# Moving operands of U, query and V at other addresses, and a shorter first ranking round

## The chip, the cores and the metric

The kernel runs on one core of a Trainium2 chip. The metric is device time in microseconds of one execution, the median of three runs. The result is one array of 256 tokens by 1024 features in float32.

## The reference, cut to what matters

Two transformer blocks run one after the other on 256 tokens of width 1024. Each ends in a PEER layer, and that is where the change lies:

```
qh = (t @ w_q).reshape(T, 8 heads, 2, 128)
s = einsum(qh, sub_keys)                       # 128 scores for each head and half
s_top, i_top = top_k(s, 16)
cand = s_top[..., 0, :, None] + s_top[..., 1, None, :]
best, pos = top_k(cand.reshape(..., 256), 16)
idx = i_top[0] * 128 + i_top[1]  at pos        # 16384 experts
g = softmax(best)
act = gelu(einsum(u_tab[idx], t))
y = einsum(g * act, v_tab[idx])
```

The second block does the same with its own tables and shared sub-keys. The rest (modulation, windowed attention, short convolution, latent attention, gated linear attention) is not touched.

## The kernel before, in words

The kernel doesn't gather experts. It multiplies all 16384 rows of U with all tokens, takes Gelu, multiplies by a dense matrix of gates that is zero for experts not chosen, and multiplies by all of V. A stage is made of units: 16 for the query (`wq`), 128 for U, 128 for V, each 512 KB of weights that SyncE streams into a ring of four slots. The two blocks are called b = 1 and b = 2.

Every float32 product is made from two float32r parts. The weights of a unit are split in halves of 512 columns: ScalarE casts the high part into `hl[:, slot, 0]` (L2321 in U, L2651 in V), VectorE subtracts to get the low part into `hl[:, slot, 1]` (L2324, L2661). `hl` has four such slots (HLRING), so two units. The tokens' parts are `hsplit` for U, `shifted_raw` (b = 1) or `raw_split` (b = 2) for the query, and `csplit` for V, whose slots (CRING = 4) hold the gated activations of one unit each. `hl` holds the stationary operand, the others the moving one.

`passes` (L937 to L939) multiplies high by high, low weights by high, and high weights by low, 256 columns each. A unit of U has eight feature blocks k, so 24 matmuls. `wide_passes` (L2245, L2246) does V: the high weights stream both parts of a `csplit` slot at once as 512 columns, then the low weights stream the high part, 256 columns. A unit of V has eight such pairs.

A partition's addresses are counted here in words of 4 bytes. `gbuf` begins at word 44064. `hl` begins there; `hsplit` and `csplit` share the space from word 48160 on. Remainders of the word address by 64:

```
                           high part   low part    stationary
hsplit (U)                    32          16           32   (hl)
raw_split (query, b = 2)      32          16           32   (hl)
csplit (V), slots 0 and 2     32          16           32   (hl)
csplit (V), slots 1 and 3      0          48           32   (hl)
h_parts (fill1, block 1)      32          32           32   (whi_front, ring_lo, s_lo)
mixed_hi, mixed_lo (w_out)    16          16           32   (whi_a, ring_lo)
```

Steps inside a tensor (256 words from one k to the next, 128 from one stationary block to the next) leave these remainders as they are. A slot of `csplit` is 608 words long: 256 high, 48 empty, 256 low, 48 empty.

The order of the work in U: VectorE does the low splits, and after each half unit n it calls `between(n)` (L2796), which does one step of the ranking. There are four rounds of 52 steps: 36 steps of top-k (`topk_part`) and 16 of lookup (`lookup_part`). ScalarE's Exp of a round's gates has a unit of its own in `exp_at` (L2744). The first two rounds end with `picks_ready`; for each, GpSimd then scatters 64 columns of gates to HBM, one indirect DMA at a time (L2478). TensorE turns the chosen experts at unit 105 (`TURN_UNIT`), and VectorE takes them at half unit `TAKE_SLOT` = 214. From unit 111 on, the gates of the other tokens are built with one-hot matmuls (L2554).

SyncE's queue (`peer_loads`) holds, in this order: the loads of U's units, each behind the split that frees its ring slot; the first four loads of V (L2864); a wait for the whole scatter; the first four loads of gates into `gring` (L2879); and then V's loads and gates in turn. In V, VectorE multiplies the activations by the gates (L2593), ScalarE casts the high part into `csplit` (L2649), VectorE subtracts the low part (L2655).

Of the kernel before, what the change touches and what calls it, by code (L numbers as in the profile page):

```python
# [24 lines left out]
F32R = mybir.dt.float32r  # L25
# [5 lines left out]
P = 128  # L31
D = 1024
KD = D // P
T = 256
# [16 lines left out]
HALF = UNIT // 2  # L51
HLRING = 4
CRING = 4
# [210 lines left out]
def build(nc, stream, xc, metaT, vectors, common, consts1, consts2, keys1, keys2, w_a2, out):  # L264
# [5 lines left out]
    def place(name, shape, dtype=F32, at=None):  # L270
        size = math.prod(shape[1:])
        where = top[0] if at is None else at
        t = nc.alloc_sbuf_tensor_at(name, shape, dtype, offset=4 * where)
        if at is None:
            top[0] += (size + 7) // 8 * 8
        return t, where

    ring, ring_at = place("ring", [P, RING, UNIT])
    ring_lo, _ = place("ring_lo", [P, RING, UNIT], F32R, at=ring_at)
    resid, _ = place("resid", [P, KD, T])  # L280
    s_area, s_at = place("s_area", [P, NT * HEADS * 2 * P])
    arena, arena_base = place("arena", [P, P * T])
    gbuf, gbuf_at = place("gbuf", [P, 10240])
    keybuf, keybuf_at = place("keybuf", [P, 2 * P])
    tmpbuf, _ = place("tmpbuf", [P, 2 * P])
    zeros, _ = place("zeros", [P, ZEROS])
    _, late_rest_at = place("late_rest", [P, 4 * P])

    hl, _ = place("hl", [P, HLRING, 2, HALF], F32R, at=gbuf_at)
    SHIFT = 48  # L290
    hpair, _ = place("hsplit", [P, 2, KD * T + SHIFT], F32R, at=gbuf_at + 2 * HLRING * HALF)
    hsplit = hpair[:, :, 0:KD * T].rearrange("p x (k t) -> p x k t", k=KD)
    cpair, _ = place("csplit", [P, CRING, 2, T + SHIFT], F32R, at=gbuf_at + 2 * HLRING * HALF)
    csplit = cpair[:, :, :, 0:T]
    vec_at, n_vec = offsets(VECS)
    con_at, n_con = offsets(CONSTS)
    vec, _ = place("vec", [P, n_vec])
    con, _ = place("con", [P, n_con])
    mod, _ = place("mod", [P, 48, 2])
    scale1, _ = place("scale1", [P, KD, 2])  # L300
    scale2, _ = place("scale2", [P, KD])
    small, _ = place("small", [P, 32])
    half_gate, _ = place("half_gate", [P, KD])
    twice_w, _ = place("twice_w", [P, 2, KD])
# [195 lines left out]
    acts = arena  # L500

    K = Space(gbuf, 10240)
    K.take(8192 + 2 * SHIFT)
    picks_best, gates = K.take(4, 64), K.take(4, 64)
    pos_f, rank1, rank2 = K.take(64), K.take(64), K.take(64)
    key_f, chosen = K.take(2, 64), K.take(2, 2 * 64)
# [307 lines left out]
    tiles[group_of["out1"][-KD]].each = ("mixed1_split",)  # L814

    h_full = gbuf[:, 8192:10240].rearrange("p (k t) -> p k t", k=KD)
    rpair, _ = place("raw_split", [P, 2, KD * T + SHIFT], F32R, at=s_at)
    raw_split = rpair[:, :, 0:KD * T].rearrange("p x (k t) -> p x k t", k=KD)
    ffn_root = n2[:, 0, 0:T]
    token_root = small[:, 26:28]  # L820

# [1428 lines left out]
    ITEMS = 4  # L2250
    ROUNDS = NT * HEADS // ITEMS
    ITEM_SLOTS, LOOK_SLOTS = 9, 16
    ROUND_SLOTS = ITEMS * ITEM_SLOTS + LOOK_SLOTS
    EXP_LAG = 2
    TURN_UNIT = ROUNDS * ROUND_SLOTS // 2 + 1
    TAKE_SLOT = 2 * TURN_UNIT + 4

# [194 lines left out]
    def take_turned(dve, b):  # L2452

        dve.wait_ge(S("experts_turned"), b)
        dve.tensor_copy(sel[:, 0:3, :], ps[:, 4, 0:3 * P].rearrange("p (c t) -> p c t", c=3))
        dve.tensor_scalar(sel[:, 3:5, :], ps[:, 4, P:3 * P].rearrange("p (c t) -> p c t", c=2), -1.0, None, ALU.mult)\
           .then_inc(S("sel_taken"), 1)
# [265 lines left out]
    def peer_act(act, b):  # L2723

        for s in range(UB):
            u_unit("act", act, b, 0, s, first=True, table="wq", ready=EARLY)
            if s == 2:
                entries[b].act_root(act)
        for s in range(UB):
            u_unit("act", act, b, 1, s, table="wq")  # L2730
            for k in (2 * s, 2 * s + 1):
                entries[b].act_high(act, k)
        u_loop("act", act, b, 2, NQ // UB, table="wq")
        early_hi(act, b, 0, "u")
        early_hi(act, b, 1, "u")
        if b == 2:
            take_unit(act, b, NQ // UB, -2, table="wq")
        early_hi(act, b, 2, "u")
        if b == 2:
            take_unit(act, b, NQ // UB, -1, table="wq")  # L2740
        early_hi(act, b, 3, "u")
        peer_act_scores(act, b)
        load_gelu(act, b)
        exp_at = {(i * ROUND_SLOTS + ITEMS * ITEM_SLOTS) // 2 + EXP_LAG: i for i in range(ROUNDS)}  # L2744
        for s in range(FIRST_STEP):
            u_unit("act", act, b, 0, s, first=True, ready=HLRING)
            if s in exp_at:
                i = exp_at[s]
                act.wait_ge(S("gates_shifted"), ROUNDS * (b - 1) + i + 1)
                act.activation(gates[:, i, :], gates[:, i, :], ACT.Exp).then_inc(S("gates_exp"), 1)  # L2750
        first = groups_of(0)
        act_hots(act, b, first[0])
        u_unit("act", act, b, 0, FIRST_STEP)
        for g in first[1:]:
            act_hots(act, b, g)
        take_unit(act, b, 0, FIRST_STEP - 1)
        for step in range(STEPS):
            s = FIRST_STEP + step
            u_unit("act", act, b, 0, s + 1, take=False)
            if step:  # L2760
                now = groups_of(step)
                act_hots(act, b, now[0])
                for g in groups_of(step - 1):
                    act_keep_late(act, b, g)
                for g in now[1:]:
                    act_hots(act, b, g)
            take_unit(act, b, 0, s)
        v_loop("act", act, b)

    def peer_dve(dve, b):  # L2770
        def entered(n):
            if n == EARLY:
                entries[b].dve_invert(dve)
        def scaled(n):
            entries[b].dve_scale(dve, n)
            if n >= 2:
                entries[b].dve_low(dve, n - 2)
        for s in range(UB):
            u_unit("dve", dve, b, 0, s, first=True, table="wq", ready=EARLY, extra=entered)
        for s in range(UB):  # L2780
            u_unit("dve", dve, b, 1, s, table="wq", extra=scaled)
        for k in (KD - 2, KD - 1):
            entries[b].dve_low(dve, k)
        u_loop("dve", dve, b, 2, NQ // UB, table="wq")
        early_lo(dve, b, 0, "u")
        early_lo(dve, b, 1, "u")
        if b == 1:
            take_query(dve, NQ // UB, -2)
        early_lo(dve, b, 2, "u")
        if b == 1:  # L2790
            take_query(dve, NQ // UB, -1)
        entries[b].dve_keep(dve)
        early_lo(dve, b, 3, "u")
        dve.wait_ge(S("peer_s_copied"), 8 * b)

        def between(n):  # L2796
            i, step = divmod(n, ROUND_SLOTS)
            if i < ROUNDS and step < ITEMS * ITEM_SLOTS:
                topk_part(dve, i, *divmod(step, ITEM_SLOTS))
            elif i < ROUNDS:  # L2800
                lookup_part(dve, b, i, step - ITEMS * ITEM_SLOTS)
            if n == TAKE_SLOT:
                take_turned(dve, b)
        for s in range(FIRST_STEP):
            u_unit("dve", dve, b, 0, s, extra=between, ready=HLRING)
        first = groups_of(0)
        for g in first[:-1]:
            dve_hots(dve, b, g)
        u_unit("dve", dve, b, 0, FIRST_STEP)
        dve_hots(dve, b, first[-1])  # L2810
        for step in range(STEPS):
            if step:
                for g in groups_of(step - 1):
                    dve_multiply(dve, b, g)
                for g in groups_of(step):
                    dve_hots(dve, b, g)
            u_unit("dve", dve, b, 0, FIRST_STEP + step + 1)
        v_loop("dve", dve, b)

        used = halves(b + 1, "wq") + HLRING * b  # L2820

        def add_half(k, part):
            src = ps[:, k, part * T:(part + 1) * T]
            if b == 1:
                return dve.scalar_tensor_tensor(resid[:, k, :], src, mod[:, 40 + k, 0:1], resid[:, k, :],
                                                ALU.mult, ALU.add)
            return dve.tensor_tensor(resid[:, k, :], src, resid[:, k, :], ALU.add)
        for k in range(KD + 1):
            half, n = divmod(k, KD // 2)
            if k < KD:  # L2830
                if n < KD // 2 - 1:
                    dve.wait_ge(S("bank_final"), (b - 1) * (KD - 2) + half * (KD // 2 - 1) + n + 1)
                else:
                    dve.wait_ge(S("split_used"), used - 2 + 2 * half)
                add_half(k, 0).then_inc(S("half_added"), 1)
            if k > 0:
                dve.wait_ge(S("half_added"), (b - 1) * KD + k)
                add_half(k - 1, 1).then_inc(S("peer_out"), 1)
# [332 lines left out]
```

## Time and profile before

| | us |
|---|---|
| median of three runs | 2235.26 (2229.96 to 2235.33) |
| profiled execution | 2233.44 |
| its span | 2231.6 |
| TensorE busy | 2190.0 (98%) |
| VectorE busy | 1690.9 (76%) |
| ScalarE busy | 1305.3 (58%) |
| GpSimd busy | 445.3 (20%) |

The span is the time from the first to the last instruction. The mean granted TensorE clock is 0.997 of full speed. A matmul's shown duration is longer than the distance to the next one's start, since matmuls are pipelined: for a stage's pace, starts have to be compared.

### The profile page before, as it was taken

The page shows a single profiled execution, that of the slowest core. Times are in us where ns is not written, and L with a number is a line of the kernel's source. Part 1 is how long each engine was busy: PE and PEld are TensorE (multiplying, and loading weights), DVE is VectorE, ACT ScalarE, POOL GpSimd, SP SyncE. Part 2 cuts the span into 40 slices and gives each one's busy share as a digit, 9 for nine tenths or more (in the row PEclk, how much of TensorE's full clock was granted, in tenths as well). Part 3 has the DMA queues.
Part 4 walks back from the last instruction along what each step waited for, and adds up shares of the span by engine and source line. Part 5 has one row for each costly group of instructions (what it writes and reads, how often), then busy time and mean ns, then how long its engine had stood idle before and what let it go on. Part 6 is the DMA issues. An engine that isn't in the chain of part 4 may idle for free.

```text
span 2231.6 us, 48254 instructions
## 1 busy us (share of the span) xinstructions
PE 2190.0 (98%) x15536; PEld 2019.4 (90%) x15536; DVE 1690.9 (76%) x3690; ACT 1305.3 (58%) x2727; POOL 445.3 (20%) x277
## 2 busy tenths in 40 slices
PE   8999999999999999999999999999999999999999
PEld 3788899999999888888879989999999998888888
DVE  4787768888879777777656866768888798777777
ACT  3477455555578555555555564655555586555554
POOL 0000000666675000000000000001767681000000
PEclk9999999999999999999999999999999999999999
DMA  8777445776764666666455434546777755666665
GB/s 331 260 232 244 176 147 187 189 185 182 189 147 126 213 213 214 215 213 212 157 170 162 150 111 145 199 162 187 184 188 185 188 124 156 213 213 213 215 213 169
DMA packets 191119, 422.88 MB, mean 189 GB/s; under 512 B 54289, under 2 KB 88337, under 8 KB 190625
## 3 DMA queue, kind: packets, MB, share of 16 engines
q1 hardware_dynamic: 150112, 413.73, 56.1%
q0 software_dynamic: 36864, 0.15, 4.6%
q10 hardware_dynamic: 4032, 7.64, 0.9%
q8 instruction: 56, 0.92, 0.2%
q14 instruction: 55, 0.44, 0.1%
HBM read 403.48 MB, written 17.96 MB: 189 GB/s over the span
## 4 chain that ended last, share of the span: by engine, by line
PE 92%; DVE 3%; ACT 2%; issue 1%; DMA 1%; POOL 0%; DVEq 0%; ACTq 0%; POOLq 0%
PE ps L2245 21%; PE ps L939 16%; PE ps L937 16%; PE ps L938 15%; PE ps L2246 11%; PE ps L962 5%; PE ps L2554 3%; PE ps L1868 1%; PE ps L1846 1%; DMA ring<-stream 1%; PE ps L2277 1%; PE ps L2168 1%; DVE ring_lo L615 1%; ACT arena L680 1%; PE ps L1860 1%
## 5 line engine op out<-in xcount | busy, mean ns | idle before, releaser
L2245 PE MATMUL ps<-csplit,hl 128*128 128x512 f32 x2048 | 711.9, 393 | 5.1 <-issue 4.1
L2478 POOL DMA_INDIRECT gates<-gbuf,picks_at x256 | 440.6, 1721 | 917.1 <-issue 487.7
L937 PE MATMUL ps<-hsplit,hl 128*128 128x256 f32 x2048 | 577.2, 282 | 0.0
L939 PE MATMUL ps<-hsplit,hl 128*128 128x256 f32 x2048 | 576.1, 281 | 0.0
L938 PE MATMUL ps<-hsplit,hl 128*128 128x256 f32 x2048 | 573.3, 280 | 0.0
L2246 PE MATMUL ps<-csplit,hl 128*128 128x256 f32 x2048 | 572.7, 280 | 0.0
L2321 ACT CAST hl<-ring 128x512 fp32r<-128x512 f32 x562 | 342.6, 619 | 286.1 <-PE ps L939 259.2
L2324 DVE TENSOR_TENSOR hl<-ring,hl 128x512 fp32r<-128x512 f32 x562 | 385.2, 691 | 111.0 <-ACT hl L2321 74.6
L2245 PEld LDWEIGHTS ps<-csplit,hl 128*128 128x128 f32 x2048 | 385.4, 188 | 91.1 <-issue 4.4
L2661 DVE TENSOR_TENSOR hl<-ring,hl 128x512 fp32r<-128x512 f32 x508 | 351.0, 692 | 69.8 <-ACT hl L2651 57.0
L2246 PEld LDWEIGHTS ps<-csplit,hl 128*128 128x128 f32 x2048 | 387.3, 189 | 0.0
L937 PEld LDWEIGHTS ps<-hsplit,hl 128*128 128x128 f32 x2048 | 386.4, 189 | 0.0
L938 PEld LDWEIGHTS ps<-hsplit,hl 128*128 128x128 f32 x2048 | 385.9, 188 | 0.0
L939 PEld LDWEIGHTS ps<-hsplit,hl 128*128 128x128 f32 x2048 | 384.7, 188 | 0.0
L2651 ACT CAST hl<-ring 128x512 fp32r<-128x512 f32 x508 | 314.4, 619 | 75.7 <-PE ps L2246 75.7
L2649 ACT CAST csplit<-arena 128x256 fp32r (+1 forms) x256 | 103.9, 406 | 235.1 <-DVE arena L2593 219.5
L2655 DVE TENSOR_TENSOR csplit<-arena,csplit 128x256 fp32r<-128x256 f32 x256 | 109.0, 426 | 122.8 <-ACT csplit L2649 122.7
L2359 ACT ACTIVATE arena<-ps 128x256 f32<-128x256 f32 (+1 forms) x272 | 103.0, 379 | 16.1 <-PE ps L939 16.0
L938 PE MATMUL ps<-n_hi,ring_lo 128*128 128x256 f32 (+1 forms) x352 | 100.3, 285 | 0.0
L2943 POOL MEMSET arena<- 128x1024 f32 x1 | 1.0, 951 | 424.3 <-PE ps L939 424.3
L687 DVE TENSOR_REDUCE arena<-arena 128x128 f32<-128x1024 f32 x32 | 62.2, 1948 | 17.6 <-ACT arena L680 17.6
L2593 DVE TENSOR_TENSOR arena<-arena,gring 128x128 f32 (+1 forms) x256 | 72.7, 284 | 2.8 <-DMA gring<-gates 2.7
(418 smaller groups left out, 3464.6 us busy)
## 6 DMA issues: line engine op xcount, KB each, us to landing
ring<-stream SPq DMA_DIRECT2D x675, 512.0 KB
s_area<-stream SPq DMA_DIRECT2D x48, 512.0 KB, 5.3
gates<-zeros SPq DMA_DIRECT2D x32, 512.0 KB, 5.0
gring<-gates SPq DMA_DIRECT2D x256, 64.0 KB, 3.1
gates<-gbuf,picks_at POOLq DMA_INDIRECT x256
arena<-xc ACTq DMA_DIRECT2D x2, 1024.0 KB, 15.5
arena<-keys ACTq DMA_DIRECT2D x2, 1024.0 KB, 7.0
gbuf<-consts ACTq DMA_DIRECT2D x1, 1120.0 KB, 5.3
```

The source lines that it names most:

```text
L937: pe.matmul(out_ap, w[0], m[0], start=start, stop=False)
L938: pe.matmul(out_ap, w[1], m[0], start=False, stop=False)
L939: return pe.matmul(out_ap, w[0], m[1], start=False, stop=stop)
L962: mm = pe.matmul(ps[0:t.rows, t.bank, 0:t.cols], lhs, rhs, start=(t.start and i == 0), stop=(t.stop and i == last))
L2245: pe.matmul(ps[:, bank, :], w_hi, m_both, start=start, stop=False)
L2246: return pe.matmul(ps[:, bank, 0:T], w_lo, m_both[:, 0, :], start=False, stop=stop)
L2321: eng.copy(hl[:, hslot, 0, :], raw).then_inc(S("split_hi"), 1)
L2324: eng.tensor_tensor(hl[:, hslot, 1, :], raw, hl[:, hslot, 0, :].bitcast(F32), ALU.subtract)\
L2478: pool.indirect_dma_start(out=cells, out_offset=bass.IndirectOffsetOnAxis(ap=picks_at[:, i, c:c + 1], axis=0), in_=gates[:, i, c:c + 1], i ...
L2651: eng.copy(hl[:, hslot, 0, :], slot(unit)[:, part]).then_inc(S("split_hi"), 1)
L2655: ins = eng.tensor_tensor(csplit[:, cslot, 1, :], acts[:, c], csplit[:, cslot, 0, :].bitcast(F32), ALU.subtract)
L2661: eng.tensor_tensor(hl[:, hslot, 1, :], slot(unit)[:, part], hl[:, hslot, 0, :].bitcast(F32), ALU.subtract).then_inc(S("split_lo"), 1)
```

## The change

Four edits:

- `hsplit` and `raw_split` lose the 48 empty words between high and low part; the whole tensor begins 48 words (192 bytes) later. The low part stays where it was, the high part moves.
- `csplit` loses its empty words, so that both parts of a slot are one run of 512 words; it begins 32 words (128 bytes) later.
- The small tiles behind `hsplit` begin 48 words earlier.
- In the first 32 half units of U, VectorE does an additional ranking step after every eighth one (LEAD = 4 of them). From then on each step comes four half units earlier. The Exp of each round is put two units earlier.

The remainders by 64 after it: `hsplit` and `raw_split` 16 for both parts, `csplit` 0 for both parts of each slot, `hl` 32 as before.

```diff
@@ -288,10 +288,8 @@
     SHIFT = 48
-    hpair, _ = place("hsplit", [P, 2, KD * T + SHIFT], F32R, at=gbuf_at + 2 * HLRING * HALF)
-    hsplit = hpair[:, :, 0:KD * T].rearrange("p x (k t) -> p x k t", k=KD)
-    cpair, _ = place("csplit", [P, CRING, 2, T + SHIFT], F32R, at=gbuf_at + 2 * HLRING * HALF)
-    csplit = cpair[:, :, :, 0:T]
+    hsplit, _ = place("hsplit", [P, 2, KD, T], F32R, at=gbuf_at + 2 * HLRING * HALF + SHIFT)
+    csplit, _ = place("csplit", [P, CRING, 2, T], F32R, at=gbuf_at + 2 * HLRING * HALF + 32)
@@ -500,7 +498,7 @@
     K = Space(gbuf, 10240)
-    K.take(8192 + 2 * SHIFT)
+    K.take(8192 + SHIFT)
@@ -814,8 +812,7 @@
-    rpair, _ = place("raw_split", [P, 2, KD * T + SHIFT], F32R, at=s_at)
-    raw_split = rpair[:, :, 0:KD * T].rearrange("p x (k t) -> p x k t", k=KD)
+    raw_split, _ = place("raw_split", [P, 2, KD, T], F32R, at=s_at + SHIFT)
@@ -2252,6 +2249,7 @@
     EXP_LAG = 2
+    LEAD, LEAD_EVERY = 4, 8
@@ -2741,7 +2739,7 @@
-        exp_at = {(i * ROUND_SLOTS + ITEMS * ITEM_SLOTS) // 2 + EXP_LAG: i for i in range(ROUNDS)}
+        exp_at = {(i * ROUND_SLOTS + ITEMS * ITEM_SLOTS - LEAD) // 2 + EXP_LAG: i for i in range(ROUNDS)}
@@ -2794,13 +2792,20 @@
         def between(n):
+            done = n + min(n // LEAD_EVERY, LEAD)
+            ranking(done)
+            if n % LEAD_EVERY == LEAD_EVERY - 1 and n < LEAD * LEAD_EVERY:
+                ranking(done + 1)
+            if n == TAKE_SLOT:
+                take_turned(dve, b)
+
+        def ranking(n):
             i, step = divmod(n, ROUND_SLOTS)
             if i < ROUNDS and step < ITEMS * ITEM_SLOTS:
                 topk_part(dve, i, *divmod(step, ITEM_SLOTS))
             elif i < ROUNDS:
                 lookup_part(dve, b, i, step - ITEMS * ITEM_SLOTS)
-            if n == TAKE_SLOT:
-                take_turned(dve, b)
```

## Rows read from the trace of the kernel before

**Rows 1.** The page's busy table (share, count) and its chain by engine.
```profile
PE 2190.0 (98%) x15536; PEld 2019.4 (90%) x15536; DVE 1690.9 (76%) x3690; ACT 1305.3 (58%) x2727; POOL 445.3 (20%) x277
...
PE 92%; DVE 3%; ACT 2%; issue 1%; DMA 1%; POOL 0%; DVEq 0%; ACTq 0%; POOLq 0%
```
**Rows 2.** Groups by line, V's wide matmuls: count | busy us, mean ns | idle before.
```profile
L2245 PE MATMUL ps<-csplit,hl 128*128 128x512 f32 x2048 | 711.9, 393 | 5.1 <-issue 4.1 <-DVE hl L2661 1.0
```
**Rows 3.** Timeline (start us, duration us), first matmuls of U's units 10 and 70, block 2.
```profile
1505.99 0.28 PE L937 MATMUL ps<-hsplit,hl 128*128 128x256 f32 x1
...
1675.59 0.28 PE L937 MATMUL ps<-hsplit,hl 128*128 128x256 f32 x1
```
**Rows 4.** Timeline, first matmuls of V's units 10 and 70, block 2.
```profile
1900.22 0.39 PE L2245 MATMUL ps<-csplit,hl 128*128 128x512 f32 x1
...
2066.22 0.39 PE L2245 MATMUL ps<-csplit,hl 128*128 128x512 f32 x1
```
**Rows 5.** Timeline, one tile of fill1, first passes of k = 1 and 7.
```profile
156.66 0.28 PE L937 MATMUL ps<-h_parts,whi_front 128*128 128x256 f32 x1
...
158.82 0.28 PE L937 MATMUL ps<-h_parts,whi_front 128*128 128x256 f32 x1
```
**Rows 6.** Timeline, one tile of w_out, first passes of k = 1 and 7.
```profile
1406.49 0.28 PE L937 MATMUL ps<-mixed_hi,whi_a 128*128 128x256 f32 x1
...
1408.61 0.28 PE L937 MATMUL ps<-mixed_hi,whi_a 128*128 128x256 f32 x1
```
**Rows 7.** Timeline, wide V matmuls of units 60 (slot 0) and 61 (slot 1).
```profile
2038.56 0.39 PE L2245 MATMUL ps<-csplit,hl 128*128 128x512 f32 x1
...
2039.25 0.39 PE L2245 MATMUL ps<-csplit,hl 128*128 128x512 f32 x1
...
2041.33 0.40 PE L2245 MATMUL ps<-csplit,hl 128*128 128x512 f32 x1
...
2042.03 0.39 PE L2245 MATMUL ps<-csplit,hl 128*128 128x512 f32 x1
...
2042.38 0.39 PE L2245 MATMUL ps<-csplit,hl 128*128 128x512 f32 x1
...
2042.71 0.39 PE L2245 MATMUL ps<-csplit,hl 128*128 128x512 f32 x1
...
2044.09 0.39 PE L2245 MATMUL ps<-csplit,hl 128*128 128x512 f32 x1
```
**Rows 8.** Timeline, VectorE early in U, and TensorE's first matmul of unit 4.
```profile
333.33 0.09 DVE L2392 MATCH_VALUE_LOAD picks_pos<-gbuf,keybuf 128x8 f32 x1
...
334.28 0.69 DVE L2324 TENSOR_TENSOR hl<-ring,hl 128x512 fp32r<-128x512 f32 x1
...
337.08 0.28 PE L937 MATMUL ps<-hsplit,hl 128*128 128x256 f32 x1
```
**Rows 9.** Windows: length, then PE, PEld, DVE, ACT, POOL busy; clock, DMA share, GB/s.
```profile
335.00:345.00 10.00, 10.00 (x87) 10.00 (x87) 8.72 (x28) 5.54 (x12) 0.00 (x0) 1.00 0.60 203
...
690.00:700.00 10.00, 10.00 (x89) 10.00 (x89) 10.00 (x24) 9.31 (x27) 8.76 (x5) 1.00 0.46 107
...
720.00:722.00 2.00, 2.00 (x8) 1.71 (x7) 0.40 (x3) 0.56 (x2) 0.00 (x0) 0.50 0.41 72
```
**Rows 10.** Timeline around the step from U to V, block 1, by engine.
```profile
706.09 1.65 POOL L2478 DMA_INDIRECT gates<-gbuf,picks_at  x1 [0.30 <-issue]
...
714.00 1.86 SPq L2879 DMA_DIRECT2D gring<-gates  x4
...
716.39 0.28 PE L939 MATMUL ps<-hsplit,hl 128*128 128x256 f32 x1
...
716.71 0.38 ACT L2359 ACTIVATE arena<-ps 128x256 f32<-128x256 f32 x1 [3.20 <-PE ps L939]
...
717.05 0.66 DVE L2593 TENSOR_TENSOR arena<-arena,gring 128x128 f32<-128x128 f32 x2 [1.18 <-DMA gring<-gates]
...
718.53 0.69 PE L2245 MATMUL ps<-csplit,hl 128*128 128x512 f32 x1 [1.86 <-issue]
```

## The prediction

> **What bounds the kernel now.** I read the page's busy table and chain first: TensorE is busy 98% of the span and carries 92% of the chain that ended last [rows 1]. Next the groups by line: the wide V matmuls alone are 2048 instructions [rows 2]. PE being full, the question is the distance from one matmul's start to the next, not the duration shown of one (393 ns for a wide one, which overlaps its neighbours). So I read starts from the timeline.
>
> U: 60 units lie between the starts 1505.99 and 1675.59 [rows 3]. That is 169.60/60 = 2.8267 us a unit of 24 matmuls, 353.3 ns for three passes, 117.8 ns each. V: 60 units lie between 1900.22 and 2066.22 [rows 4]: 2.7667 us a unit of 8 pairs, 345.8 ns a pair. At this clock (2.4 GHz, granted 1.00) the bare columns are 768 for three narrow passes and for a pair alike, 320.0 ns. So 33.3 ns in U and 25.8 ns in V are something else, and the change can only aim at that. U holds 2 x 128 x 2.8267 = 723.6 us, V 2 x 128 x 2.7667 = 708.3 us.
>
> **What an address does.** The same three-pass sequence runs at two paces. For h_parts 18 matmuls lie between 156.66 and 158.82 [rows 5]: 2.16/18 = 120.0 ns, 360.0 for three. For mixed_hi and mixed_lo, 18 lie between 1406.49 and 1408.61 [rows 6]: 2.12/18 = 117.8 ns, 353.3 for three. In the first, moving and stationary data all have remainder 32 (word address by 64). In the second, both moving parts have 16 and all stationary blocks 32. U has 32 (high), 16 (low) and 32 (stationary) and goes at the pace of the second. I take it that the 6.7 ns are lost only where everything is aligned. The remainder by 64 is my reading of these cases, not shown as a law.
>
> **U's parts together (hsplit).** After the change high and low have remainder 16 and the stationary blocks 32. That is the case of [rows 6], to the word of the remainder. So: 353.3 ns now [rows 3], 353.3 ns then; gain 0. Bounds: if sharing a remainder is what makes [rows 5] slow, three passes go to 360.0. That is +53.3 ns a unit, 256 x 53.3 = +13.7 us. On the good side no U-like row is shorter. I take the same size with the other sign as the bound, -13.7 us, cut below for the end of U. I take 0, because [rows 6] is the nearest row; what differs there is only where the tiles lie (mixed in the arena, hsplit beside hl).
>
> **The query's parts (raw_split).** Only block 2's 16 query units use it, with the same remainders as hsplit before and after. Value 0, bounds +-16 x 53.3 ns = +-0.9 us. Block 1's query (shifted_raw) isn't touched.
>
> **V's coefficients in one run (csplit).** Two things change: the seam of 48 words inside the wide pass goes, and all four slots get remainder 0 where they had 32, 0, 32, 0. The trace has both kinds of slot side by side [rows 7]. Unit at 2038.56 (slot remainder 32): from its third pair at 2039.25 to the next unit at 2041.33 are 6 pairs in 2.08 us, 346.7 ns each. Unit at 2041.33 (slot remainder 0): from 2042.03 to 2044.09 are 6 pairs in 2.06 us, 343.3 ns each. But its first two pairs take 2042.03 - 2041.33 = 0.70 us, 350 ns each. Both kinds have the seam. So the slot remainder is worth 3.3 ns a pair, and the step from one kind to the other costs about 13 ns a unit. With all slots alike I expect 8 x 343.3 = 2.747 us a unit, 0.020 less: 256 x 0.020 = **-5.1 us**. The seam I cost at nothing: the aligned slots lose 26.7 ns over bare columns in two weight loads, as much per load as h_parts without any seam (40.0 ns in three). Bounds: the remainder-0 slot alternates. Its shorter pairs, as 2042.38 to 2042.71 [rows 7], are about 340 ns; if all became that, 8 x 340 = 2.720 us, -11.9 us. If all went like the aligned slot, 8 x 346.7 = 2.773 us, +1.7 us. I take -5.1, the mean of the slot that stays as it is.
>
> **The first ranking round.** In the first 32 half units DVE does one more ranking step every eighth, so all later steps come 4 half units (5.7 us) earlier. The work is the same, moved. Queued behind an extra step are DVE's low splits for PE. A step of the costly kind took 334.28 - 333.33 = 0.95 us, and the split begun at 334.28 ends at 334.97, while PE begins with it at 337.08 [rows 8]: 2.1 us in hand. The first extra step goes just before that split, so 1.1 us stay. From 335 to 345 us DVE is busy 8.72 of 10 [rows 9]; eleven microseconds with 1.4 of idle time hold one extra step. ACT's Exp is put 2 units earlier with its data and costs no more. Cost 0; uncovered it would be 4 steps of 0.95 us a block, +7.6 us in both, and I see no reason for that.
>
> What could be early by it is the scatter. POOL's last indirect DMA starts at 706.09. SP waits for the scatter only after its last V load, and reaches the gates' loads at 714.00 [rows 10]: its DMA issues till then are bound to DVE's low splits of U's last units, since the V loads wait for ring slots. POOL has been done for six microseconds. PE ends U at 716.39 and begins V at 718.53; between lie ACT's Gelu at 716.71 and DVE's first gate multiply at 717.05, released by the gates' landing. Nothing in this chain comes sooner when POOL is done sooner. Gain 0. After the gap PE runs for a while at the lower clock (1.2 GHz; granted 0.50 from 720 to 722 [rows 9]), and that stays as the gap stays. PE's turning of the experts stays at unit 105.
>
> The small tiles behind hsplit move by 192 bytes; DVE and ACT read them off PE's path, cost 0.
>
> **Sum.** 0 + 0 - 5.1 + 0 = -5.1 us. The profiled execution took 2233.44 us (span 2231.6), 1.8 us under the median 2235.26 of three; its difference applied to the median gives **2230.1 us**.
>
> **A rule that speaks against the change.** The Trainium skill, "SBUF — State Buffer", section "Who interferes with whom", gives TensorE two independent read ports, moving and weights, and says it waits for nobody; "TensorE: Matmul & The Clock Gate", section "Back-to-back issue gap", prices a warm matmul by its columns alone, N/2.4 + 2.5 ns. By these no address matters, a pair would be 325.0 ns (an estimate from that page) and the edit would move nothing. The trace disagrees: [rows 5] and [rows 6] have one shape and two paces, and [rows 7] shows two paces inside V at 346.7 and 343.3 ns.
>
> **The rivals.**
> 1. *U gets faster too*, because the two high passes leave the stationary remainder. For it: in U two passes of three still share 32 with the weights. Against it: in [rows 6] none does, and the pace is U's. Price: one more step of the size between [rows 5] and [rows 6], 6.7 ns in three passes. In the last 16 units of each block DVE is busy 10.00 of 10 [rows 9], so only 2 x 112 units gain: -11.9 us. The query gives -0.9. With V's -5.1: 2217.4 us.
> 2. *Aligned again, slower.* If U's present pace comes from high and low being apart, putting them together brings back the 120.0 ns of [rows 5]. Place: every U unit and block 2's query. Price +13.7 + 0.9, less V's 5.1: +9.5, 2244.8 us. It decides as soon as a U unit is over 2.847 us (256 x 0.020 = 5.1). Against it: [rows 6] have high and low alike and no loss.
> 3. *Addresses don't matter in V*, the two kinds of slot being due to something else (the hl slots they are paired with, which don't move): no change, 2235.3 us. For it: each kind of csplit slot always meets the same hl slots.
>
> **How the numbers follow.** This measurement tells about 0.3% (6.7 us) from no change, so the bound of "faster" is 2228.6. Forecast case (V alone gains) 0.50, and as its own bound reaches -11.9 I give 0.20 of it to faster and 0.30 to the same. Rival 1: 0.25, faster. Rival 3: 0.12, the same. Rival 2: 0.13, slower. Together 0.45, 0.42, 0.13. The range 2215 to 2241 holds the forecast case, rival 3 and most of rival 1; the full price of rival 2 is left out.
>
> **What would show it.** In the changed profile: a U unit of 2.827 us (rival 1: 2.773, rival 2: 2.880); V units all of one length, 2.747, where now they alternate; no idle time of PE ahead of U's matmuls between 326 and 400 us; POOL's last DMA 5 to 6 us earlier and PE's first V matmul no closer to its last U one. The prediction is wrong if the U unit moves at all, or if V's units still differ by slot.

## The result, and the profile after

The median of 20 runs is 2237.16 us (2230.42 to 2244.10), against 2233.06 (2229.96 to 2240.95) in 20 runs of the kernel before beside them. The ratio is 1.0017, 95% interval [1.0009, 1.0025]: 0.2% slower (4.1 us by the medians), inside the 0.3% that I had called the same. I had forecast 2230.1 us, which was 5.1 us less than a median before of 2235.26. The profiled execution took 2236.17 us, its span is 2234.4 (before 2233.44 and 2231.6).

The page's busy table and chain, and the group of V's wide matmuls (they answer to [rows 1, 2]):

```profile
PE 2189.1 (98%) x15536; PEld 2012.4 (90%) x15536; DVE 1691.4 (76%) x3690; ACT 1306.2 (58%) x2727; POOL 445.1 (20%) x277
...
PE 91%; DVE 4%; ACT 2%; issue 1%; DMA 1%; POOL 0%; DVEq 0%; ACTq 0%; POOLq 0%
...
L2242 PE MATMUL ps<-csplit,hl 128*128 128x512 f32 x2048 | 722.3, 395 | 7.7 <-issue 6.7
```

The shares don't give the change away: TensorE is busy 98% as before, and a wide matmul is shown 2 ns longer. The wide group's busy time does: it was 711.9 us in [rows 2] and is 722.3. The matmuls of this group overlap, so its busy time is nearly the length of V. What happened in U shows in the starts only. Timeline of the changed kernel (start us, duration us): first matmuls of U's units 10 and 70 in block 1, then in block 2, then of V's units 10, 70 and 71 in block 2 ([rows 3, 4] before).

```profile
355.96 0.28 PE L934 MATMUL ps<-hsplit,hl 128*128 128x256 f32 x1
...
525.56 0.28 PE L934 MATMUL ps<-hsplit,hl 128*128 128x256 f32 x1
...
1512.31 0.28 PE L934 MATMUL ps<-hsplit,hl 128*128 128x256 f32 x1
...
1675.64 0.28 PE L934 MATMUL ps<-hsplit,hl 128*128 128x256 f32 x1
...
1898.07 0.40 PE L2242 MATMUL ps<-csplit,hl 128*128 128x512 f32 x1
...
2066.60 0.40 PE L2242 MATMUL ps<-csplit,hl 128*128 128x512 f32 x1
...
2069.41 0.40 PE L2242 MATMUL ps<-csplit,hl 128*128 128x512 f32 x1
```

- U in block 1: 169.60/60 = 2.827 us a unit, as in [rows 3].
- U in block 2: 163.33/60 = 2.722, and 2.720 without the two units that are told of below: 113.3 ns a matmul where [rows 3] have 117.8. Two blocks of one execution, the same code and addresses, two paces. I call them the long and the short rhythm.
- V: 168.53/60 = 2.809 us a unit, 0.042 more than in [rows 4]. The last two rows are one unit apart, 2.81. All units are alike now, as I had said, but at the wrong length: 351 ns a pair, where the best slot of [rows 7] has 343.3.

The profiled time holds two large opposite terms. V: 256 x 0.0422 = +10.8 us. U in block 2: from its first to its last matmul 378.7 us instead of 390.7, -12.0. Of the rest, a part is the step from U to V in block 2. Timeline of the changed kernel, SyncE's loads of gates, GpSimd's last scatter and TensorE's last U and first V matmul:

```profile
1860.85 2.93 POOL L2476 DMA_INDIRECT gates<-gbuf,picks_at  x1 [2.64 <-issue]
...
1865.32 1.75 SPq L2884 DMA_DIRECT2D gring<-gates  x4
...
1863.75 0.28 PE L936 MATMUL ps<-hsplit,hl 128*128 128x256 f32 x1
1868.54 0.77 PE L2242 MATMUL ps<-csplit,hl 128*128 128x512 f32 x1 [4.51 <-issue]
```

With U 12 us shorter, TensorE starts its last matmul of U (1863.75) as the last scatter ends (1863.78). SyncE loads gates at 1865.32, and V begins 4.8 us after U (2.5 before in the same block: last U matmul at 1868.34, first V matmul at 1870.85, gates loaded from 1865.99). That takes 2.3 us back. The span grew by 2.8 us, and 10.8 - 12.0 + 2.3 is 1.1. The other 1.7 us are nearly all (1.9) ahead of block 1's U, whose first matmul is at 327.62 instead of 325.69; this start moves from one execution to the next (325.7 to 332.7 in those profiled below).

### The profile page after: what moved, and what is told of

The parts are those of the page before. It is cut to its first block, busy times and chain, and to the rows that moved or that the text cites. A ratio compares the mean times of both kernels' runs of the same rounds, so it can differ in the third digit from the quotient of the medians.

```text
span 2234.4 us, 48254 instructions
## 1 busy us (share of the span) xinstructions
PE 2189.1 (98%) x15536; PEld 2012.4 (90%) x15536; DVE 1691.4 (76%) x3690; ACT 1306.2 (58%) x2727; POOL 445.1 (20%) x277
## 4 chain that ended last, share of the span: by engine, by line
PE 91%; DVE 4%; ACT 2%; issue 1%; DMA 1%; POOL 0%; DVEq 0%; ACTq 0%; POOLq 0%
PE ps L2242 21%; PE ps L934 15%; PE ps L936 15%; PE ps L935 15%; PE ps L2243 11%; PE ps L959 5%; PE ps L2552 3%; PE ps L1865 1%; PE ps L1843 1%; DMA ring<-stream 1%; PE ps L2275 1%; PE ps L2165 1%; DVE ring_lo L613 1%; ACT arena L678 1%; PE ps L1857 1%
## 5 line engine op out<-in xcount | busy, mean ns | idle before, releaser
L2242 PE MATMUL ps<-csplit,hl 128*128 128x512 f32 x2048 | 722.3, 395 | 7.7 <-issue 6.7
L2243 PE MATMUL ps<-csplit,hl 128*128 128x256 f32 x2048 | 580.5, 283 | 0.0
L2357 ACT ACTIVATE arena<-ps 128x256 f32<-128x256 f32 (+1 forms) x272 | 103.2, 379 | 13.2 <-PE ps L936 12.1
```

Of the source, the lines that this page charges most:

```text
L2242: pe.matmul(ps[:, bank, :], w_hi, m_both, start=start, stop=False)
L2243: return pe.matmul(ps[:, bank, 0:T], w_lo, m_both[:, 0, :], start=False, stop=stop)
```

## Experiments

The interval in brackets is 95%, always against the kernel before in the same comparison. V's and U's paces are the distance between the first matmuls of units 10 and 70, divided by 60.

### The parts of the change, each alone

`e1_v_only`: before, with the change's `csplit` (one run of 512 words, remainder 0).

```diff
-    cpair, _ = place("csplit", [P, CRING, 2, T + SHIFT], F32R, at=gbuf_at + 2 * HLRING * HALF)
-    csplit = cpair[:, :, :, 0:T]
+    csplit, _ = place("csplit", [P, CRING, 2, T], F32R, at=gbuf_at + 2 * HLRING * HALF + 32)
```

> The kernel before with the V edit alone (csplit in one run, remainder 0). Theory A (the V edit by itself is what lengthens V): V units go from 2.767 to 2.809 us in both blocks, +10.8 us, U units stay at 2.827 us in both. Theory B (V's new pace comes from the other edits or from chance): V stays at 2.767 and the time is that of before.

2245.89 us, ratio 1.0054 [1.0039, 1.0070]. V 2.809 in both blocks, U 2.827 in both. The timeline of its V, units 10 and 70 of block 2 (168.53/60 = 2.809):

```profile
1905.30 0.40 PE L2244 MATMUL ps<-csplit,hl 128*128 128x512 f32 x1
...
2073.83 0.40 PE L2244 MATMUL ps<-csplit,hl 128*128 128x512 f32 x1
```

V's edit alone costs 10.8 us by its pace, 12.2 by the medians.

`e2_u_only`: before, with the change's `hsplit` and `raw_split`.

```diff
-    hpair, _ = place("hsplit", [P, 2, KD * T + SHIFT], F32R, at=gbuf_at + 2 * HLRING * HALF)
...
+    hsplit, _ = place("hsplit", [P, 2, KD, T], F32R, at=gbuf_at + 2 * HLRING * HALF + SHIFT)
...
+    raw_split, _ = place("raw_split", [P, 2, KD, T], F32R, at=s_at + SHIFT)
```

> The kernel before with the U and query edit alone. Theory A (the new addresses allow two rhythms, 2.827 and 2.720 us a unit, and chance at a stage's beginning picks one for the stage): V stays at 2.767; U units are either 2.827 or 2.720 throughout a block, so the time is that of before, or 11 to 12 us less for each block in the short rhythm; single runs fall into clusters about 12 us apart. Theory B (the short rhythm of block 2 belongs to block 2's own code or to the ranking edit): block 1 at 2.827 always, block 2 as the changed kernel or as before.

2228.07 us (2217.02 to 2239.32 in 12 runs), ratio 0.9971 [0.9954, 0.9988]. V as before. In the profiled execution U is long in block 1 up to unit 105, where TensorE turns the experts, and short in units 107 to 110 after it (2.720); in block 2 it is short throughout. So the short rhythm belongs neither to block 2 nor to the ranking edit. The 12 times don't fall into groups 12 us apart, as the expectation had it. The timeline of this kernel, units 10 and 70 of block 2, then the end of U, the scatter, the gates and V's first matmul:

```profile
1503.06 0.28 PE L935 MATMUL ps<-hsplit,hl 128*128 128x256 f32 x1
...
1666.26 0.28 PE L935 MATMUL ps<-hsplit,hl 128*128 128x256 f32 x1
...
1854.37 0.28 PE L937 MATMUL ps<-hsplit,hl 128*128 128x256 f32 x1
...
1858.20 1.54 POOL L2476 DMA_INDIRECT gates<-gbuf,picks_at  x1 [1.94 <-issue]
...
1861.24 1.75 SPq L2877 DMA_DIRECT2D gring<-gates  x4
...
1864.53 0.77 PE L2243 MATMUL ps<-csplit,hl 128*128 128x512 f32 x1 [9.89 <-issue]
```

163.20/60 = 2.720. But the scatter ends only at 1859.7 (1858.20 + 1.54), and V begins 10.2 us after U. Here and in the changed kernel the gates' loads follow the scatter's end by 1.5 us, so it is the scatter that they wait for. In the changed kernel the gap was 4.8 us. I read the 5.4 us between them as the ranking edit's worth when U is short; it is one execution of each. Counted from U's first matmul, the scatter ends after 384.0 us here and after 378.8 there, and the same end moves from 372.8 to 382.1 in block 1 of the four long-U kernels without the ranking edit (before, e1, e3, e4).

`e8_rank_only`: before, with the change's `LEAD`, `between` and `exp_at` alone.

```diff
+    LEAD, LEAD_EVERY = 4, 8
...
+            done = n + min(n // LEAD_EVERY, LEAD)
+            ranking(done)
+            if n % LEAD_EVERY == LEAD_EVERY - 1 and n < LEAD * LEAD_EVERY:
+                ranking(done + 1)
```

> Before with the ranking edit alone, all addresses as before. Theory of the prediction (cost hidden, gain none): within 1 us of before, U units 2.827, gap from the last U to the first V matmul 2.1 to 2.5 us as before, the last indirect DMA of the scatter 5 to 6 us earlier. Rival 1 (the extra steps delay the low splits that TensorE waits for in the first 16 units): idle of TensorE ahead of U's matmuls between 326 and 400 us, +1 to +7.6 us. Rival 2 (an earlier scatter shortens the gap to V): gap below 2 us, -0.5 to -2 us.

2233.28 us, ratio 1.0003 [0.9993, 1.0013]: no effect that can be told from none, as predicted. TensorE has no idle time ahead of U's matmuls from 326 to 400 us. Its timeline, block 1: the last scatter DMA, the gates' loads, the last U and the first V matmul (compare [rows 10]):

```profile
698.93 1.66 POOL L2479 DMA_INDIRECT gates<-gbuf,picks_at  x1 [0.30 <-issue]
...
716.11 1.86 SPq L2887 DMA_DIRECT2D gring<-gates  x4
...
718.49 0.28 PE L939 MATMUL ps<-hsplit,hl 128*128 128x256 f32 x1
720.79 0.67 PE L2245 MATMUL ps<-csplit,hl 128*128 128x512 f32 x1 [2.02 <-issue]
```

The gap from U to V is 2.3 us in both blocks, where it was 2.1 and 2.5. GpSimd's last issue is 7.2 us earlier than in [rows 10], but block 1 doesn't show that this is the edit's doing: e1, without the edit, has its last scatter as early (371.1 us after U's first matmul, like e8). Block 2 does. There the scatter ends 371.8 us after U's first matmul in e8, and 380.1 to 380.3 in the four kernels without the edit that have a long U.

### What in V's edit costs: the missing gap, or the remainders?

`e3_v_seam`: before, all slots at remainder 0, the 48 empty words kept.

```diff
-    cpair, _ = place("csplit", [P, CRING, 2, T + SHIFT], F32R, at=gbuf_at + 2 * HLRING * HALF)
-    csplit = cpair[:, :, :, 0:T]
+    cpair, _ = place("csplit", [P, CRING, 640], F32R, at=gbuf_at + 2 * HLRING * HALF + 32)
+    csplit = cpair[:, :, 0:608].rearrange("p c (x t) -> p c x t", x=2)[:, :, :, 0:T]
```

> The kernel before, csplit with the 48-word seam kept, but all four slots at remainder 0 (a slot is 640 words). Theory A (V's loss comes from closing the seam): V units at 2.747 to 2.767 us, no loss, perhaps 5 us gained. Theory B (the loss comes from remainder 0 in all slots): V units at 2.809 us, +10.8 us.

2229.02 us, ratio 0.9981 [0.9967, 0.9995]. The timeline of its V, units 10 and 70 of block 2:

```profile
1900.03 0.39 PE L2245 MATMUL ps<-csplit,hl 128*128 128x512 f32 x1
...
2064.83 0.39 PE L2245 MATMUL ps<-csplit,hl 128*128 128x512 f32 x1
```

164.80/60 = 2.747 us, the predicted unit to the nanosecond, and 4.6 us off the median for a predicted 5.1. The step was right for another edit than the one made.

`e4_v_run32`: one run of 512 words, but `csplit` 32 words earlier, so remainder 32 in all slots.

```diff
-    cpair, _ = place("csplit", [P, CRING, 2, T + SHIFT], F32R, at=gbuf_at + 2 * HLRING * HALF)
...
+    csplit, _ = place("csplit", [P, CRING, 2, T], F32R, at=gbuf_at + 2 * HLRING * HALF)
```

> The kernel before, csplit in one run of 512 words per slot at remainder 32, the same as the stationary blocks. Theory A (a closed seam costs): V units at 2.8 us or more. Theory B (remainder 0 is what costs, the seam does nothing): V units at 8 x 346.7 ns = 2.773 us, +1.7 us.

2245.11 us, ratio 1.0045 [1.0027, 1.0063]. V has 2.827 in block 1 and 2.773 in block 2: a second place with two rhythms.

`e7_seam_back`: the changed kernel with V as in e3.

```diff
-    csplit, _ = place("csplit", [P, CRING, 2, T], F32R, at=gbuf_at + 2 * HLRING * HALF + 32)
+    cpair, _ = place("csplit", [P, CRING, 640], F32R, at=gbuf_at + 2 * HLRING * HALF + 32)
+    csplit = cpair[:, :, 0:608].rearrange("p c (x t) -> p c x t", x=2)[:, :, :, 0:T]
```

> The change with one thing undone: the 48 empty words between V's high and low part are back, all slots at remainder 0 (as in e3). hsplit, raw_split and the ranking as in the change. Theory (closing the seam is the whole loss): V units 2.747 us in both blocks where the change has 2.809, that is 256 x 0.062 = 15.9 us less than the change. U units 2.827 or 2.720, each block by its entry; against before -5 us with no block in the short rhythm, about -15 with one, -25 with both. Mean expected 2233 - 5 - 10 = 2218, spread 2208 to 2228. Rival (the short rhythm of U or the earlier ranking costs V something): V above 2.76, total within 3 us of before.

2226.74 us (2213.85 to 2239.09), ratio 0.9964 [0.9947, 0.9980]. V 2.747 in both blocks; the whole of V's loss is gone. V's units 10 and 70 of block 2 (164.80/60 = 2.747):

```profile
1896.89 0.39 PE L2243 MATMUL ps<-csplit,hl 128*128 128x512 f32 x1
...
2061.69 0.39 PE L2243 MATMUL ps<-csplit,hl 128*128 128x512 f32 x1
```

U had been expected to give more than it did. It entered the short rhythm in block 2 and lost it after 15 units. This kernel's timeline there, VectorE's low split first, then two weight loads, then TensorE's last matmul of unit 15 and the first two of unit 16:

```profile
1521.30 0.69 DVE L2323 TENSOR_TENSOR hl<-ring,hl 128x512 fp32r<-128x512 f32 x1
...
1521.84 0.19 PEld L937 LDWEIGHTS ps<-hsplit,hl 128*128 128x128 f32 x1
...
1522.11 0.19 PEld L935 LDWEIGHTS ps<-hsplit,hl 128*128 128x128 f32 x1
...
1521.95 0.28 PE L937 MATMUL ps<-hsplit,hl 128*128 128x256 f32 x1
1522.14 0.36 PE L935 MATMUL ps<-hsplit,hl 128*128 128x256 f32 x1
1522.33 0.28 PE L936 MATMUL ps<-hsplit,hl 128*128 128x256 f32 x1
```

The next weight load would be due at 1521.95 (one every 0.11 us); the split ends at 1521.99, the load begins at 1522.11. TensorE has caught up with VectorE. The next two matmuls each start 0.19 us after the one before instead of 0.11, and from unit 17 on the units are 2.827 long. In the changed kernel the two distances at the same place are 0.16 and 0.19, units 15 and 16 together take 0.13 us more than two of 2.720, and the rhythm survives; in e2, without extra ranking steps, the block runs through it at 2.720. That the stop ended the rhythm is read from its place in time; no run made the stop alone.

Up to here I read the cause as the missing gap. But e3 and e7 put the low part at remainder 48 as well. A gap of 64 words leaves both parts at remainder 0, but as two runs, and tells the readings apart. `e9_seam64` is the changed kernel with

```diff
-    csplit, _ = place("csplit", [P, CRING, 2, T], F32R, at=gbuf_at + 2 * HLRING * HALF + 32)
+    cpair, _ = place("csplit", [P, CRING, 640], F32R, at=gbuf_at + 2 * HLRING * HALF + 32)
+    csplit = cpair[:, :, 0:640].rearrange("p c (x t) -> p c x t", x=2)[:, :, :, 0:T]
```

> The changed kernel with one thing altered: 64 empty words between V's high and low part instead of none, slots 640 words long, so both parts of every slot keep remainder 0 as in the change, but are two runs. This parts two readings of the loss. Theory S (what costs is that the 512 columns are one run without a gap): V units 2.747 us as with the seam of 48, total as the run with the seam put back, some 2227 us. Theory R (what costs is that low and high part have the same remainder, the gap being only how they came to differ): V units 2.809 us as in the change, total near 2237 us. U at 2.827 or 2.720 in either.

2245.24 us, ratio 1.0053 [1.0032, 1.0073]. Its timeline, V's units 10 and 70 of block 2:

```profile
1908.31 0.40 PE L2243 MATMUL ps<-csplit,hl 128*128 128x512 f32 x1
...
2076.84 0.40 PE L2243 MATMUL ps<-csplit,hl 128*128 128x512 f32 x1
```

168.53/60 = 2.809, the changed kernel's pace with a gap of 64 words. Theory S fell: the gap as such is worth nothing. With the high part at 0, the low part's remainder makes the difference: 48 gives 2.747, 0 gives 2.809. It is also the one direct test of the divisor 64: the low part moved by 64 words and the pace stayed. The time missed the expectation (near 2237) by 8 us; U is long in both blocks of the profiled execution up to unit 105, which fits, but there are only four executions.

### Other pairs of remainders

Each is the changed kernel with other offsets and gaps of `csplit`, `hsplit` and `raw_split`; the pairs are in the expectations. For `hsplit` at 32/0, for example:

```diff
-    hsplit, _ = place("hsplit", [P, 2, KD, T], F32R, at=gbuf_at + 2 * HLRING * HALF + SHIFT)
+    hpair, _ = place("hsplit", [P, 2, KD * T + 32], F32R, at=gbuf_at + 2 * HLRING * HALF)
+    hsplit = hpair[:, :, 0:KD * T].rearrange("p x (k t) -> p x k t", k=KD)
```

The first two, in four and ten executions:

> The changed kernel with other remainders: hsplit and raw_split 32 words after their base, so both parts have remainder 0 (16 in the change), csplit with its 48 empty words back and both parts of every slot at remainder 16 (low part 0), instead of one run at 0. Theory A (TensorE locks into one of two rhythms because of the pair moving 16, weights 32): at 0 and 32 there is no reason for two, U goes at one pace in both blocks. V: if what counts is only that all slots are alike and the two parts are not one run, a V unit is 2.747 us as in e3, not 2.809. Theory B (the two rhythms belong to any arrangement in which both moving parts share a remainder other than the weights'): U at 2.720 or 2.827 again, each block its own. Theory C (remainder 0 is what makes V fast): V at 16 is 2.77 or more. Total against before: A with short rhythm 2233 - 5 - 25 = 2203, A with long rhythm 2228; B between; C 5 us more than each.

> The changed kernel with hsplit and raw_split at remainder 48 for both parts, csplit with the 48 empty words back and the high part at 48, the low part at 32 (the weights' own remainder). Theory A: one pace in U, either always 2.720 or always 2.827 us a unit. Theory B: both, by block. V: theory C' (a low part at the weights' remainder 32 costs, as the slots of before with 32 did, 346.7 ns a pair) gives 2.773 us a unit, +1.7 us over before in both blocks; if the shared remainder does not matter, 2.747, -5.1 us.

2244.95 us [1.0036, 1.0065] and 2235.74 us [1.0001, 1.0019]. The first can be added up: U 2.848 (224 x 0.0213 = 4.8 us more than before), V 2.791 (256 x 0.0244 = 6.2), sum 11.0, measured 11.7. U keeps one pace in it, as theory A had it, but a longer one than any forecast. In e6 V is 2.773, and U is 2.827 up to unit 105 of both blocks. After the turn it is short, here from unit 107 to unit 110 of block 2 (8.16/3 = 2.720):

```profile
1779.73 0.28 PE L935 MATMUL ps<-hsplit,hl 128*128 128x256 f32 x1
...
1787.89 0.28 PE L935 MATMUL ps<-hsplit,hl 128*128 128x256 f32 x1
```

One execution each, for the paces (e10 and e11, then e12 to e15, then e17):

> The changed kernel with other remainders throughout, for the paces alone: V high part 0, low part 16 (seam of 16 words); hsplit high 16, low 0; raw_split high 48, low 16. Theory S (any seam will do in V): V units 2.747 us. Theory R (the pair of remainders sets it): another pace than 2.747, since 0 and 48 gave 2.747, 48 and 32 gave 2.773, 16 and 0 gave 2.791. U: if the two parts must share remainder 16 for the second rhythm, one pace in both blocks, 2.827 or longer; a pace of 2.720 in both blocks would be the version to build.

> As the run before it, for the paces alone: V high part 32, low part 16 in all four slots (two of four slots had this before; 346.7 ns a pair there, 2.773 us a unit if a slot's pace is its own); hsplit high 48, low 16; raw_split high 0, low 16. For V both theories say 2.773; a value of 2.747 would mean that only the alternation of the slots cost. U: one pace in both blocks by the theory that only 16 with 16 has two.

> The changed kernel at other remainders, for the paces alone: V high 16, low 48; hsplit high 16, low 48; raw_split high 0, low 48. If the low part's remainder sets V's pace, 2.747 us a unit as with 0 and 48; if the distance does (here 32, there 48), 2.77 to 2.80. U: one pace if only 16 with 16 has two.

> The same with V high 32, low 48; hsplit high 0, low 48; raw_split high 16, low 32. Low part's remainder: 2.747. If a high part at the weights' own remainder 32 costs 3.3 ns a pair whatever the low part: 2.773 (as with 32 and 16).

> The same with V high 48, low 48 (64 empty words between); hsplit high 32, low 48; raw_split high 32, low 0. Low part's remainder: 2.747. If equal remainders are what costs (0 with 0 gave 2.809, 32 with 32 gave 2.827 and 2.773): 2.80 or more.

> The same with V high 48, low 16; hsplit high 16, low 32; raw_split high 48, low 0. Low part's remainder: 2.773 to 2.800, as the other two pairs with 16; if the distance sets it (32 as in 16 with 48), the same pace as the run with 16 and 48. U at 2.720 in both blocks under any of these pairs would be the version to build.

> For the paces alone: V high 32, low 0; hsplit high 0, low 32; raw_split high 48, low 32. If high part at the weights' remainder with low at 0 is short in wide passes too, V units under 2.747; if narrow and wide have nothing to do with each other, 2.773 to 2.827, as most pairs. U 2.827 to 2.88.

They took 2243.03 (e10), 2236.18, 2239.68, 2241.95, 2256.00, 2250.48 (e11 to e15) and 2251.11 us (e17).

All paces read, us a unit, high part / low part, the stationary blocks always at 32 (a value for each rhythm seen; a star marks one seen only in units 107 to 110, after the turn of the experts):

```
V    0/48   2.747              32/0    2.800
    32/16   2.773              32/48   2.800
    16/48   2.773               0/0    2.809 (gap 0 or 64)
    48/32   2.773              48/48   2.827
    16/0    2.791              48/16   2.827
     0/16   2.800              32/32   2.827, 2.773

U   16/16   2.827, 2.720       32/16, 16/48, 32/48, 16/32   2.827
    32/0    2.827, 2.800        0/0    2.848
     0/48   2.853, 2.809       16/0    2.850, 2.853*
    48/48   2.827, 2.720*       0/32   2.880
    48/16   2.827, 2.809*

query   0/16   2.907, 2.827     48/0    2.827     48/32   2.853
```

No single rule that I tried holds: not the low part's remainder (48 gave 2.747, 2.773, 2.800 and 2.827), not the distance (16/48 and 48/16: 2.773 and 2.827), not equality alone (0/0 and 48/48 are long, but so is 48/16), and narrow and wide passes rank the pairs differently. It is a table, and its logic stays open.

### Versions built from the table

`e16_best`: the changed kernel with V 0/48 (the diff of e7), U and query 32/0 (the diff above, and the same for `raw_split`).

> The changed kernel with the two best pairs of remainders seen: V high 0, low 48 (2.747 us a unit in two runs), hsplit and raw_split high 32, low 0 (2.800 in the query units of one run). If a pair's pace is the same in the query and in U: U units 2.800 us in both blocks and in all executions, 2 x 112 x 0.027 = 6.0 us less than before, query 16 x 0.027 = 0.4, V 5.1: 11.5 us under before, some 2222 us, with a narrow spread (2219 to 2225). If the query's pace is one of two rhythms: some blocks at 2.827 or more, 2222 to 2232.

2224.36 us (2218.94 to 2227.92 in 6 runs), ratio 0.9960 [0.9945, 0.9976]. V 2.747. Its timeline, U's units 10 and 70 in block 1, then in block 2:

```profile
355.69 0.28 PE L937 MATMUL ps<-hsplit,hl 128*128 128x256 f32 x1
...
523.69 0.28 PE L937 MATMUL ps<-hsplit,hl 128*128 128x256 f32 x1
...
1500.19 0.28 PE L937 MATMUL ps<-hsplit,hl 128*128 128x256 f32 x1
...
1669.80 0.28 PE L937 MATMUL ps<-hsplit,hl 128*128 128x256 f32 x1
```

2.800 and 2.827: the second case of the expectation, 32/0 has two rhythms. In block 1 the short one ended at unit 105, where TensorE turns the experts; in block 2 it began there (units 107 to 110 at 2.800). The turn can switch the rhythm either way.

`e18_lead6`: e7 with the extra ranking steps closer together and earlier (`LEAD_EVERY = 6`), so that none stands near unit 15.

```diff
-    LEAD, LEAD_EVERY = 4, 8
+    LEAD, LEAD_EVERY = 4, 6
```

> The run with V's seam put back, with one constant changed: an extra ranking step after every sixth half unit instead of every eighth (LEAD_EVERY = 6). If the fourth extra step is what disturbs the short rhythm: units 15 and 16 at 2.720 each in a block that has it, the rhythm kept to the end of U (block 378.5 us instead of 388.3), total 2218 to 2222 median. Rival (VectorE has too little idle time in the short rhythm for four extra steps wherever they are, and closer together is worse): the loss comes at an earlier unit (8 to 12), the rhythm is lost there, total as before this edit, 2226.7 or above. If no profiled block enters the short rhythm, only the total speaks.

2226.84 us (2214.29 to 2229.75), ratio 0.9963 [0.9947, 0.9979], as e7. Neither profiled block entered the short rhythm before the turn at unit 105, so whether the fourth extra step is what ends it stays open: seen is only that the two short blocks with it lost time at units 15 and 16 and the one without it didn't.

e7, e16 and e18 are 0.4% faster than the kernel before, where the changed one is 0.2% slower; their intervals don't part them.

## Why the prediction was wrong

- **The failed step is "The seam I cost at nothing", in V's coefficients.** I had the remainders 0 and 48 of the good slots before me, and read them as "slot remainder 0". The change makes them 0 and 0. The gap between the parts is indeed worth nothing (e9); what closing it does to the low part's remainder costs. The term was -5.1, bounds -11.9 to +1.7; measured +10.8 by the pace, outside them. My bounds came from the slots of [rows 7], neither of which has the pair that the change makes.
- The other half of the step held: all slots at 0/48 run at 343.3 ns a pair, 2.747 a unit, and the 13 ns for the step from slot to slot go (e3).
- **U, gain 0**: wrong as well. "The prediction is wrong if the U unit moves at all", and in the profiled execution it moved in one block of two, by 0.107, twice what rival 1 had. Up to the turn, block 1 was long in all five profiled executions of 16/16 and block 2 was short in two, and in a third (e7) until unit 15. What picks the rhythm is open. [Rows 6] showed the long rhythm of just this pair (16/16); I took one tile's pace for the pair's pace. The bound of 13.7 us covers the 12.0 of one block, not of two. In e2 the edit's gain by the medians is 5.6 us; its profiled execution won 12.1 in U of block 2 and gave 7.7 back in the longer gap to V. My 723.6 us for U also counted 128 equal units a block. Units 111 to 127, in which gates are built too, take some 4.6 us, and U's first and last matmul lie 390.7 us apart; the sum did not use this figure.
- **The query, 0**: wrong too, by little. In the changed kernel ten of its 16 units (3 to 6 and 9 to 14, counted from 0) are 2.720. First matmuls of units 9 and 15 (16.32/6 = 2.720):

```profile
1458.05 0.28 PE L934 MATMUL ps<-raw_split,hl 128*128 128x256 f32 x1
...
1474.37 0.28 PE L934 MATMUL ps<-raw_split,hl 128*128 128x256 f32 x1
```

  From its first to its last matmul the query takes 44.9 us instead of 46.0, 1.1 less, which is past the bound of 0.9.
- **Ranking, cost 0 and gain 0**: right where U is in the long rhythm (e8). In the short one neither held in the executions profiled: the cover of [rows 8] is used up (the stop at unit 16 in e7), and the earlier scatter goes with a gap 5.4 us shorter (10.2 in e2, 4.8 in the change). I had written that nothing in the chain comes sooner when GpSimd is done sooner; that was the chain of a U of 390 us.
- **The rivals**: rival 3 (addresses don't matter in V) is refuted by e1 and e3, rival 2 by U's units at 16/16, which run at 2.827 or 2.720 wherever they are steady. The rule against the change gave 325.0 ns a pair at any address; the paces measured go from 343.3 to 353.3 with the address. The case that came true, U gains and V loses, I didn't have. That its sum is near 0 is chance: by the medians +12.2 (e1), -5.6 (e2) and 0.0 (e8) make +6.6, measured +4.1, each term uncertain by 2 to 4 us.

## What to carry to other kernels

Before an address is changed, write down the full pair of remainders (high and low, not only the slot's base) that the edit makes, and look for a row with just that pair; if there is none, the cost has no bound from the trace. A pace read in one stretch may be one of two that the same code can take: compare both blocks and several tiles before it is called the pace of an address. When a saturated engine gets faster, walk again through what was late by less than the gain: the producer next to it, and the last transfer before the following stage.

## What the runs showed of the hardware

- TensorE's back-to-back pace for matmuls of one shape depends on the addresses of the moving operand: 128 x 256 in three passes from 113.3 ns (2.720/24) to 120.0 (2.880/24) each, a pair of 512 and 256 columns from 343.3 to 353.3 ns (2.747/8, 2.827/8), all at a granted clock of 1.00. Why the address matters is open.
- Some pairs have two rhythms that last for up to a hundred units and more: 16/16, 32/0 and 0/48 in U, 32/32 in V. 48/48 and 48/16 showed a second one in U's units 107 to 110 alone. Once (e7) the short rhythm ended at two distances of 0.19 us from one matmul to the next instead of 0.11; 0.16 and 0.19 in the changed kernel did not end it.
- The clock after the gap between U and V. Windows of e7, 0.9 us after V's first matmul in block 1 and 0.7 us in block 2 (columns as in [rows 9]):

```profile
721.00:724.00 3.00, 3.00 (x11) 2.54 (x10) 1.73 (x5) 0.92 (x2) 0.00 (x0) 0.50 0.45 153
1870.00:1873.00 3.00, 3.00 (x19) 2.67 (x18) 2.17 (x5) 1.55 (x3) 0.00 (x0) 1.00 0.41 112
```

The gap was 2.48 us ahead of the first (717.65 to 720.13), 2.53 ahead of the second (1866.79 to 1869.32), both from last U to first V matmul. The first time TensorE was granted 0.50 (1.2 GHz), the second time 1.00 (2.4 GHz). V's first unit took 4.43 us and 2.85. I had forecast that the lower clock stays as the gap stays; here it doesn't follow from the gap alone.
